# Applying the first norm's inverse root behind the matmuls: one kernel, one change, one prediction

## What is computed

```
n  = x * rsqrt(mean(x*x) + eps) * g_mix
z  = n @ w_in + b_in        # q, k, v, u, bg, cg (512 wide), ga, gc (1024)
ya = attention(rms_norm(q), rms_norm(k), v)
yc = bg * short_conv(cg * u)
m  = sigmoid(ga) * (ya @ w_pa) + sigmoid(gc) * (yc @ w_pc)
h  = x + m @ w_o
```

## Time and profile before

| | |
|---|---|
| median of 3 runs | 1948.33 us (1947.48 to 1949.45) |
| profiled execution | 1950.33 us, of which the span is 1948.2 us |
| busy: PE, DVE, ACT, POOL | 1888.7 (97%), 917.8 (47%), 637.3 (33%), 139.8 (7%) |
| chain that ended last | PE 86%, DVE 7%, DMA 5%, ACT 1% |

### The profile page before, as it was taken

How to read it: one execution, slowest core, us unless ns; L and a number is a source line. 1 busy time by engine, 2 the same in 40 slices (tenths; PEclk the granted TensorE clock), 3 DMA queues, 4 the chain that set the end, 5 groups by cost and what they waited for, 6 DMA issues and landing times.

```text
span 1948.2 us, 31374 instructions
## 1 busy us (share of the span) xinstructions
PE 1888.7 (97%) x13564; PEld 1565.8 (80%) x13564; DVE 917.8 (47%) x1611; ACT 637.3 (33%) x1187; POOL 139.8 (7%) x120
## 2 busy tenths in 40 slices
PE   7999999989999999999899999999999999999998
PEld 6866788866666666669789999999867898888898
DVE  5755434233333332247873322447866564423355
ACT  6344323121111011126432222234466543222242
POOL 0022000110000000000000000004222000000001
PEclk9999999999999999999899999999999999999999
DMA  5222242689999999963112232334321213332333
GB/s 190 87 76 76 84 170 96 263 349 429 429 429 430 428 428 428 428 273 99 54 46 87 87 100 83 90 108 142 109 66 55 85 47 108 94 110 82 104 124 115
DMA packets 57149, 345.16 MB, mean 177 GB/s; under 512 B 7168, under 2 KB 7808, under 8 KB 44976
## 3 DMA queue, kind: packets, MB, share of 16 engines
q1 hardware_dynamic: 53184, 334.15, 46.5%
q0 software_dynamic: 3504, 8.54, 1.3%
q10 hardware_dynamic: 320, 0.43, 0.1%
HBM read 343.09 MB, written 4.19 MB: 178 GB/s over the span
## 4 chain that ended last, share of the span: by engine, by line
PE 86%; DVE 7%; DMA 5%; ACT 1%; issue 1%; POOL 0%; DVEq 0%; SPq 0%; ACTq 0%; POOLq 0%
PE bank L487 57%; PE bank L703 9%; PE bank L727 6%; DMA e<-in_we 4%; PE bank L738 1%; PE bank L543 1%; PE bank L739 1%; PE bank L1137 1%; DVE wlo L1321 1%; PE bank L1084 1%; PE bank L920 1%; PE bank L690 1%; PE bank L1056 1%; PE bank L881 1%; PE bank L560 1%
## 5 line engine op out<-in xcount | busy, mean ns | idle before, releaser
L1321 DVE TENSOR_TENSOR wlo<-raw,whi 128x1024 fp32r<-128x1024 f32 x230 | 286.7, 1253 | 127.2 <-ACT whi L2322 123.5
L2322 ACT CAST whi<-raw 128x1024 fp32r<-128x1024 f32 x231 | 239.7, 1043 | 127.3 <-PE bank L487 110.3
L703 PE MATMUL bank<-e,xT 128*64 128x256 f32 x2048 | 234.7, 382 | 1.0 <-DVE xT L1594 1.0
L703 PEld LDWEIGHTS bank<-e,xT 128*64 128x64 f32 x2048 | 143.1, 137 | 80.4 <-issue 11.2
L487 PE MATMUL bank<-nhi,whi 128*128 128x272 f32 (+1 forms) x672 | 191.6, 285 | 1.1 <-DVE sl L1850 0.6
L487 PE MATMUL bank<-nhi,wlo 128*128 128x272 f32 (+1 forms) x672 | 191.2, 284 | 0.0
L487 PE MATMUL bank<-nlo,whi 128*128 128x272 f32 (+1 forms) x672 | 190.6, 284 | 0.0
L487 PE MATMUL bank<-n1hi,whi 128*128 128x512 f32 (+1 forms) x448 | 163.0, 364 | 0.0
L487 PE MATMUL bank<-n1lo,whi 128*128 128x512 f32 (+1 forms) x448 | 160.8, 359 | 0.0
L487 PE MATMUL bank<-n1hi,wlo 128*128 128x512 f32 (+1 forms) x448 | 160.7, 359 | 0.0
L487 PEld LDWEIGHTS bank<-nhi,whi 128*128 128x128 f32 x672 | 127.2, 189 | 2.0 <-DVE sl L1850 0.8
(11 more groups left out here) (397 smaller groups left out, 3768.4 us busy)
## 6 DMA issues: line engine op xcount, KB each, us to landing
e<-in_we SPq DMA_DIRECT2D x94, 2048.0 KB, 22.1
raw<-in_w_down SPq DMA_DIRECT2D x64, 512.0 KB, 3.6
raw<-in_w_gate SPq DMA_DIRECT2D x44, 512.0 KB, 3.5
raw<-in_w_up SPq DMA_DIRECT2D x44, 512.0 KB, 3.6
raw<-in_w_q SPq DMA_DIRECT2D x12, 512.0 KB, 4.4
B<-in_rel POOLq DMA_DIRECT2D x8, 512.0 KB, 4.8
raw<-in_w_gc SPq DMA_DIRECT2D x8, 512.0 KB, 3.6
raw<-in_w_ga SPq DMA_DIRECT2D x8, 512.0 KB, 4.2
```

The source lines that it names most:

```text
L703: p = e.matmul(b[64 * hf:64 * hf + 64, 0:256], x[:, k, :], W[:, k, 256 * hf:256 * hf + 256], start=(k == 0), stop=(k == 7))
L1321: e.tensor_tensor(wlo[wslot(u)][:], raw[u % NRAW][:], whi[wslot(u)][:].bitcast(F32), ALU.subtract).then_inc(*hit("dve_low", ("lo", u)))
L2322: e.copy(whi[wslot(u)][:], raw[u % NRAW][:]).then_inc(*hit("act_high", ("hi", u)))
```

## The change

- PE transposes the raw x (`xt`) as it lands. ACT still reads the banks times g_mix into `xhi`, DVE makes `xlo`; both are now unscaled. The same banks are then copied to `hT` (ACT k = 0, 4 to 7, DVE 1 to 3) and free after that. The second transposition is gone.
- The inverse root is made in the side of this; DVE multiplies it into a diagonal (`dg`), four PE matmuls with ones spread it over the partitions (L606 of the changed kernel), ACT copies that to `rb`.
- Each product is multiplied by `rb` on DVE as it is read out: `x_scaled` (into SBUF, for q, k, cg, gc, ga) and `x_scaled_there` (back into its bank, for u, bg). ACT's bias, sigmoid and square then start from SBUF. V takes the factor of its token as a scalar in its one readout.
- Tiles 0 and 1 are read out together behind tile 1. HEAD_LAG is 4. The load of weight unit 0 and its split go ahead of x.

```diff
-    HEAD_LAG = 2
+    HEAD_LAG = 4
...
+        def x_scaled(to, *key):
+
+            w.wait_ge(*at("free", "rb x"))
+            w.wait_ge(*at("out", *key))
+            e.tensor_tensor(to, bk(*key, 0), rb[:, 0:S], ALU.mult).then_inc(*hit("dve_out", ("free", *key, 0)))
...
+        def dve_head(i):
+            x_scaled(qk[:, i, :], "q" if i < 4 else "k", i % 4)
...
         dve_load()
-        side.add(nothing(3))
+        side.add(nothing(8))
         side.add(dve_meta())
-        side.add(nothing(14))
+        side.add(nothing(4))
         for i in range(8):
             tile(J["q" if i < 4 else "k"], i % 4)
+            for j in (0, 1) if i == 1 else (i,) if i else ():
+                dve_head(j)
             side.add(nothing(HEAD_LAG))
             side.add(dve_head_norm(i))
-            if i == 2:
-                side.add(nothing(4))
...
+            feed(0)
+            for i in range(3):
+                x_square(i)
+            w.wait_ge(*at("vec"))
+            x_high(0)
+            x_high(1)
+            x_copy(0)
+            x_high(2)
+            x_high(3)
+            feed(1)
+            for k in range(4, 8):
+                x_high(k)
+            x_square(3)
+            for k in range(4, 8):
+                x_copy(k)
+
         def act_head(i):
             n = "q" if i < 4 else "k"
             z = qk[:, i, :]
-            w.wait_ge(*at("out", n, i % 4))
-            e.activation(z, bk(n, i % 4, 0), ACT.Identity, bias=v1("b_in", i)).then_inc(
-                *hit("act_out", ("free", n, i % 4, 0)))
+            w.wait_ge(*at("free", n, i % 4, 0))
+            e.activation(z, z, ACT.Identity, bias=v1("b_in", i)).then_inc(*hit("act_out"))
             w.wait_ge(*last("act_out"))
...
+        load(0)
         for i in range(4):
             e.dma_start(xt[:, i, :], T["x"][i * 128:(i + 1) * 128, :]).then_inc(*dma(f"d_x{i}", ("x", i)))
         for u in range(U_MOE):
-            load(u)
+            if u:
+                load(u)
```

More of the change, by code:

```diff
@@ L599, in pe_branches, with pe_spread_x @@
             side.drain()
[L601 to L608, removed]
+        def pe_spread_x():
+            b = take(("rb x",), SIDE)
+            w.wait_ge(*at("diag x"))
+            for i in range(4):
+                p = e.matmul(b[:, i * 128:(i + 1) * 128], ones, dg[:, i, :], start=True, stop=True)
+            p.then_inc(*hit("pe_norm", ("spread x",)))
+            yield
         def pe_mix():
@@ L1201, in tensor @@
         pe_load()
-        side.add(nothing(3))
+        side.add(nothing(8))
         side.add(pe_meta())
-        side.add(pe_raw_x(range(6)))
+        side.add(nothing(4))
+        side.add(pe_spread_x())
         for i in range(8):
@@ L1330, in tile, with root_x @@
                     side.tick()
+        def root_x(i):
+            y, m, u = (xs[:, n, i:i + 2] for n in range(3))
+            w.wait_ge(*at("x sq", i + 1))
+            e.tensor_scalar(m, m, 1.0 / D, EPS, ALU.mult, ALU.add).then_inc(*hit("dve_mean", ("mean", "x", i)))
+            root(e, w, y, m, u, "dve_root", "x", i)
         def dve_load():
             e.memset(epst[:], EPS).then_inc(*hit("dve_set", ("eps",)))
[L1334 to L1341, removed]
             feed(0)
+            root_x(0)
             for k in range(8):
@@ L2443, in act_mix @@
                     tile(J["ga", h], m)
-                    w.wait_ge(*at("out", "ga", k))
-                    if h:
-                        w.wait_ge(*at("m", k - 2))
-                    else:
-                        w.wait_ge(*at("yc", 3))
-                    e.activation(sg[:, m, :], bk("ga", k, 0), ACT.Sigmoid, bias=v1("b_in", 24 + k)).then_inc(
-                        *hit("act_out", ("free", "ga", k, 0)))
+                    if m:
+                        gate(k - 1)
                 for m in range(2):
@@ L2932, in scalar @@
         act_load()
-        side.add(nothing(4))
-        side.add(act_raw_x(range(6)))
-        side.add(nothing(1))
+        side.add(nothing(13))
         for i in range(8):
             tile(J["q" if i < 4 else "k"], i % 4)
-            act_head(i)
+            if i == 1:
+                w.wait_ge(*at("spread x"))
+                e.copy(rb[:, 0:S], bk("rb x")).then_inc(*hit("act_out", ("free", "rb x")))
+            for j in (0, 1) if i == 1 else (i,) if i else ():
+                act_head(j)
             side.add(nothing(HEAD_LAG))
             side.add(act_head_norm(i))
-            if i == 2:
-                side.add(act_raw_x((6, 7)))
         act_values()
@@ L2984, in pool_attention @@
             w.wait_ge(*at("turned x", 7))
+            w.wait_ge(*at("x sq", 3))
             bias(0)
```

115 lines of the change are left out of this document (68 added, 47 removed).

## The result

The changed kernel took 1965.71 us (median of 5 runs, 1965.18 to 1969.69), the kernel before 1947.54 (5 runs, 1947.31 to 1949.45): a ratio of 1.0096 (95% interval 1.0086 to 1.0107), 18.2 us more. The direction was as forecast, the size was not: 1956.2 was predicted, at most 1960.5. The profiled execution took 1965.71 us (span 1963.9).

The account below looks back on a forecast made before the run. PE was taken to bound the kernel, busy all the time from 45 to 72 and 212 to 346 us. Terms -4.4 +9.9 +0.9 +0.9 +0.6 = +7.9 us on the median 1948.33 gave 1956.2 us, range 1946 to 1960.5.

Parts of the forecast that it names:

- Behind 346 us, where I see nothing that could: Code after 346 us: nothing seen there that could give back the predicted loss; the delay stays +7.9 us.
- No cost: Conv, branches and mix, 212 to 346 us: DVE's added readout passes cost PE nothing.
- Should a readout be late by its own length it would still be in time: Branches: PE wants its banks again 2.7 us later at the shortest, against readouts of about 0.7 us.
- The ring: Heads: readout, square, sum, root, reciprocal, next readout take 7.8 us against PE's 6.34; waits 11.6, net +9.9 us.
- It waits 6.6 us: Heads: PE's wait to sum head 3, then 2.1 us for head 4 and 1.45 each for heads 5 and 6.
- The clock's term: Heads: PE's pauses lower its clock, priced at one sum at the lower level, +0.9 us (0.86).
- The start: Up to the end of tile 1: without scaling x and waiting for its root, tile 1 ends 4.4 us earlier.
- 2.5 us later by the prediction's estimate: Start: rival that the clock stays down over the transposes, rising only behind 5 us of products; 1958.7 us, chance 3%.
- The values: Behind tile 7: V's readouts stand behind reciprocal 7, so the second half waits for its bank; +0.9 us.
- the attention: Attention: an added DVE pass delays a softmax, so PE's transposes of unit 11 are late; +0.6 us.
- the heads keep pace: Heads: rival that DVE's readouts come in time, so waits of 11.6, 0.9 and 0.9 us vanish; 1942.8 us, chance 17%.

Follow-up runs that it names:

- e6: Changed kernel with 40 do-nothing instructions added at the very start of PE's program; 1965.16 us, ratio 1.0072.
- e9: Changed kernel with 40 empty PE instructions placed where PE waits anyway (start, route, experts); 1960.39 us, ratio 1.0068.
- e7: Kernel before the change with 216 do-nothing instructions added at the very start of PE's program; 1971.07 us, ratio 1.0111.
- e4: Changed kernel with the second gate's readout in the branches put ahead of the low split on DVE; 1966.61 us, ratio 1.0091.
- e2: Changed kernel with q and k read by ACT, without the first norm's factor and DVE's eight readouts; 1952.98 us, ratio 1.0025.
- e3: Changed kernel without the reciprocal of the heads' norm (q and k multiplied by the root itself); 1947.39 us, one run.
- e1: Changed kernel with the heads' norm put off by six steps instead of four (HEAD_LAG 6); 1973.73 us, ratio 1.0134.
- e11: Changed kernel with reciprocal and product of head i-2 behind readout i on DVE, HEAD_LAG 6; 1954.42 us, one run.
- e12: Changed kernel with e11's order, reciprocal 7 put off to the attention's third unit, plus e4's and e9's edits; 1945.55 us, ratio 0.9989.
- e5: Changed kernel with reciprocal and product of head i-1 moved right behind readout i on DVE; 1958.24 us, ratio 1.0050.

## Why the prediction was wrong in size

The forecast's terms add up to 7.9 us, the measured ones to 15.7. Of the 7.8 between, the heads have 1.5, the values 0.5, the branches 1.7, the route 0.9, the experts -2.2, the stretch at L920 with its clock 6.5, and what follows it -1.1. Without the 6.5 alone, the time would have been 1959.2 us, within the range.

- **"Behind 346 us, where I see nothing that could"** is the step that failed most. I counted PE's removed instructions as time saved and not as 40 places by which all later ones move. The stretch at L920 with the low clock behind it is 6.5 us of the 15.7; e6 and e9 remove it, e7 makes the stretch in the old kernel. The range held nothing for code that the change doesn't touch.
- **"No cost" for the branches failed** too: 1.7 us. "Should a readout be late by its own length it would still be in time" counted the readout's 0.69 us and not what stands ahead of it in order: a cast, `yahi`, `yalo`, a split. Before, ACT's sigmoid freed the bank with none of DVE's ahead of it. e4 gave 1.2 us of it back.
- **The ring** was right as a mechanism, and mis-sized. "It waits 6.6 us", then 2.1, 1.45, 1.45: measured 6.70, 1.74, 1.60, 1.59. But what counts is the length of its turns: 9.11, 8.16 and 8.16 us instead of three times 7.8. 0.23 us of each lie between sum and root, 1.13 instead of 0.90. I had read the 0.90 from the chain, whose row of the sum begins 0.16 us behind the timeline's (68.23 and 68.07). That the waits still add up to 11.6 is luck: the turns were longer, but PE's own work between the waits was as well. e2 and e3 take the ring away from two sides.
- **The clock's term** came out as priced, 0.96 us against 0.86. In the first turn the root started 2.09 us behind the sum instead of 1.13, since the sum ran at the lower level. PE's own work lost more there, 1.5 us (from the sum's start to the fourth product behind it 3.10 us instead of 1.56), but part of that only shortened the next wait. The window from this sum on, and the sum with its wait in the next turn:

```profile
51.89:54.96 3.07, 3.07 (x5) 1.81 (x6) 0.26 (x1) 1.48 (x2) 0.00 (x0) 0.50 0.59 171
```
```profile
51.89 2.06 PE bank L525 x2
...
53.98 0.69 ACT hsq L2417
...
61.00 1.11 PE bank L525 x2
```

- **The start** was right, -4.4 forecast and -4.4 measured, but in part by luck. The transposes took from 6.58 to 12.3 us:

```profile
L510 PE MATMUL bank<-cst,xt x7: 417/417/417, 8.7 to 10.0; 128*128 128x128 f32 x7
L510 PE MATMUL bank<-cst,xt x15: 273/273/358, 10.4 to 12.0; 128*128 128x128 f32 x15
```

  The durations tell the level here: the clock column of the windows reads 1.00 throughout, because the trace's record of the granted clock only begins at 10.58 us. With the same start the fall in duration came at 9.6 us in e1 and at 13.1 in e3, and the end of tile 1 lay between 4.8 (e11) and 3.2 us (e3) ahead of before. The rule of the Trainium skill ("TensorE: Matmul & The Clock Gate", Part 4), by which transposes don't bring up the clock, would have made it 2.5 us later by the prediction's estimate; the trace disagrees once more, with nothing but transposes on PE when they became shorter.
- **The values**, +0.9, were +1.35; **the attention**, +0.6, was +0.6.
- **The base**: I added the sum to the median of 1948.33, and the profiled execution from which the terms are read was 2.0 us above it, while that of the changed kernel lies on its median. So the time missed by 9.5 us, where the sum of the terms missed by 7.8.
- Two slips: 50.5 less 40.68 is 9.8, not 9.9, and the range's upper end, 2 + 2 us above 1956.2, is 1960.2, not 1960.5.

Of the rivals, "the heads keep pace" was priced at 1942.8 us; e12, which makes them do so, took 1945.6.

**What stays open.** Between 410 and 873 us, the experts, the delay changed by -2.2 us in the changed kernel, but by between -3.6 (e7) and +1.1 (e4) in others, with no order that I can see; part of the difference between e9 and the changed kernel lies there. The route's +0.9 was not looked into. Whether the clock falls behind the stretch at L920 doesn't go by its length alone: 1.95 us in e11 and 2.07 in e2 brought it down, 2.03 in e7 did not. In e5 1.13 us did not. And why PE's instructions come late at just this place, of all places where a fetched piece begins, was not tried.

## What to carry to other kernels

When a readout moves to another engine, draw the whole loop of waits through every queue that it now stands in, and compare the loop with the bound engine's pace: the engine's busy time didn't tell here, since DVE was less busy when it cost 13 us. Putting a step off (e1) only moved the loss; what removed it was the order of the instructions on the engine where the loop closes (e11, e12). And ask for each new readout what stands ahead of it in order, not how long it takes.

## What the runs showed of the hardware

- 40 instructions less on PE ahead of a place made 2.3 us of idle time there, hundreds of microseconds behind the last edited line. The profile calls it "issue" and shows no releaser. On the page there is a queue of instruction fetches, q8: 109 packets and 1.79 MB, some 16 KB each. In all eight kernels with the stretch PE went on 1.2 to 1.5 us behind the landing of such a packet. Shifts by +40 and by +216 undo and make the stretch, and they add up to 256. The Trainium skill ("Vector Engine (DVE) Microarchitecture Reference", 2.1) gives every instruction 64 bytes, so by estimate a packet would hold 256; no row shows an instruction's length. That the fetch is what PE waits for is the reading that fits all of this. No row shows the wait itself, or says which engine a packet is for.
- An instruction that holds two waits already fulfilled costs PE about 0.11 us: with 176 more of them ahead of it, the first transpose began at 28.70 us in e7 and at 9.64 in e6.
- The lower clock level came behind the 6.7 us in the heads and behind most of the idle stretches of 1.95 to 2.6 us at L920, not behind the 1.2 and 1.1 us of e3 and e5.
